# A hybrid decoder step on one core: cached keys laid out on the host, early chunk loads with filler products, and fillers in the prompt attention

## The chip, the core and the metric

The kernel runs on one core of a Trainium2 chip. The core has five engines, each with an instruction stream of its own: TensorE (PE) multiplies matrices, VectorE (DVE) and ScalarE (ACT) work on rows, GpSimd (POOL) does memsets and issues indirect transfers, SyncE (SP) issues most transfers. The streams meet only at semaphores. Transfers (DMA) bring data from the chip's memory into the on-chip memory (SBUF); PE writes into eight banks of PSUM, and DVE or ACT copy from there. The metric is the time of one execution in microseconds (us). The kernel before took 1394.13 us (median of 3 runs, 1391.05 to 1395.88).

## The reference

One layer, applied to a prompt of 512 tokens and to 8 samples of 4 tokens that each have 512 cached positions (4 pages of 128):

```
z = RMSNorm(x) @ W_in                 # 1024 -> [u 512 | q 512 | k 512 | v 512]
pool:  windowed means of u minus u, a linear per group, a scale
attn:  4 heads, each head's q and k in two halves of 64:
       (softmax(q1 k1 - slope*dist) - lambda * softmax(q2 k2 - slope*dist)) @ v, then RMSNorm
       samples attend to cache_k[page_table], cache_v[page_table] and to their new keys
h = x + [pool | attn] @ W_out
y = h + MoE(RMSNorm(h))               # 32 experts, 4 per token, clamped SwiGLU
out = RMSNorm(y); also the new pool rows, keys and values
```

cache_k has the shape (1, pages, 128 positions, 4 heads, 128 features), in float32.

## The kernel before

Everything is written by hand, engine by engine; what stands in an engine's stream is executed in that order, and nothing schedules it. The 544 tokens are five tiles (four of 128 rows, one of 32). The stages that matter here, in order of time:

**Norm and input projection.** SP loads the x tiles into two halves of `raw[:, 1]` in turn. ACT sums squares (`norm1_sums`, L740 to L745), DVE scales the rows (`norm1_rows`, L1075), PE transposes the tile (`x_transposed`, L1518), and ACT and DVE split the transposed tile into a rounded high half and a low rest (`t_hi` L758, `t_lo` L1093). The weights come in 12 chunks of 256 columns, 1024 KB each (`load_pro`, L417): 8 of W_in, 4 of W_out. A chunk is split too, by ACT (`pro_hi`, L734) into `hi` and by DVE (`pro_lo`, L1071) into `lo`, each a ring of 4 slots. A unit is one chunk by one tile: 24 products of 256 columns (`three`, L1527), high by high, high by low, low by high. PE starts unit 0 when chunk 0's low half and tile 0's low half are there. ACT copies the units' results out of PSUM, and the conversions of later chunks stand between these copies in its stream (L784). Chunks are staged in `raw[:, 0]` and `raw[:, 2]`; `raw[:, 2]` also holds xn and the gains, so chunk 2 is loaded only after all x tiles are transposed (L421).

**Prompt attention** (L1622 to L1641). 16 steps, one for each query tile and head. In step i PE makes the scores of step i + 2, waits for DVE's weights of step i (`s_a`), transposes them into PSUM bank 4 + i % 2, and multiplies the transposed weights of step i - 1 by the values. DVE adds distances, finds the maximum (L1181, L1185) and mixes the two halves (L1198); ACT takes exponentials (L883) and copies the transposed weights out (L875).

**Sample attention and output projection** (L1747 to L1777). Four sample sequences at a time: `sample_group(t)` runs over 4 heads. The cached keys come as pages with positions on partitions, so PE first transposes 16 page pieces of 128 x 128 (`page_transposes`, L1656), ACT and DVE copy two banks each into `kt_s` (L909, L1230), and `sample_scores` (L1671) multiplies. Between the two groups and after them stand pieces of the output projection (`out_product`, L1710) and the value products (`sample_values`, L1702). The pages lie in `raw`: 4 sequences at a time, 16 loads of 256 KB a set, and there are four sets: keys of sequences 0 to 3 and 4 to 7, then values of both. SP asks for the next set when the last one has been read (L469 to L472): the second keys and the first values wait for page transposes (`s_kp`), the second values for the first value products (`s_vd`).

**Router, then the experts.** The weight stream of the experts (w1 and w2, 2048 KB a load) starts when the last sample values are done (L498); up to six loads are outstanding, then each waits for PE to finish with a slot.

Of the kernel before, what the change touches and what calls it, by code (L numbers as in the profile page):

```python
# [31 lines left out]
P = 128  # L32
# [7 lines left out]
H = 4  # L40
# [122 lines left out]
def build(nc, a):  # L163
# [10 lines left out]
    with ExitStack() as ctx:  # L174
# [73 lines left out]
        kt_s = [A(A_P, 4, 512), A(A_QT, 4, 512)]  # L248
# [52 lines left out]
        s_pro = {i: sem(f"projection_weights_loaded{i}") for i in (0, 2)}  # L301
# [15 lines left out]
        s_qb, s_kp, s_sss = sem("q_blocks"), sem("page_groups_transposed"), sem("sample_score_groups")  # L317
        s_kc, s_kd, s_vd = sem("page_t_out_on_scalar"), sem("page_t_out_on_vector"), sem("sample_values_done")
# [48 lines left out]
        def pro_slot(g):  # L367
            return 2 if g >= 2 and g % 2 == 0 else 0
# [40 lines left out]
        def _(sp):  # L409
# [7 lines left out]
            def load_pro(g):  # L417
                if g == 1:
                    sp.wait_ge(s_lo, 1)
                if g == 2:  # L420
                    sp.wait_ge(s_tp, NT)  # L421
                if g >= 3:
                    sp.wait_ge(s_lo, g - 1)
                src = w_in[:, :, 256 * g:256 * g + 256] if g < 8 else w_out[:, :, 256 * (g - 8):256 * (g - 8) + 256]
                sp.dma_start(raw[:, pro_slot(g), :].rearrange("p (k n) -> p k n", k=KT), src).then_inc(s_pro[pro_slot(g)], 16)
# [23 lines left out]
            load_pro(2)  # L449
# [3 lines left out]
            for g in range(3, PRO):  # L453
                load_pro(g)
# [7 lines left out]
            def load_pages(cache, b, s):  # L462
                if s == 0:
                    sp.wait_ge(s_lo, PRO)
                if s == 1:
                    sp.wait_ge(s_po, 4)
                if s == 3:
                    sp.wait_ge(s_ust, 32)
                if s in (4, 8):  # L469
                    sp.wait_ge(s_kp, s)  # L470
                if s == 12:
                    sp.wait_ge(s_vd, 1)  # L472
                for n in range(PAGES):
                    sp.dma_start(page[:, PAGES * (s % 4) + n, :],  # L474
                                 a[cache][0][bass.ds(number[b * PAGES + n], 1)].rearrange("a t h d -> (a t) (h d)")).then_inc(s_pg[s % 4], 16)
# [79 lines left out]
        def _(pool):  # L555
            pool.memset(t_hi[:, :, NTOK:640].bitcast(F32), 0.0)
# [4 lines left out]
            pool.memset(b1_parts[:], 0.0)  # L561
# [161 lines left out]
        def _(act_e):  # L723
# [5 lines left out]
            def split_hi(slot_raw, slot, loaded):  # L729

                act_e.wait_ge(s_pro[slot_raw], loaded)
                act_e.activation(hi[:, slot, :], raw[:, slot_raw, :], ACT.Copy).then_inc(s_hi, 1)  # L732
# [168 lines left out]
            def page_t(g):  # L901

                act_e.wait_ge(s_kp, g + 1)
                if g == 1:
                    act_e.wait_ge(s_qb, 2)
                if g >= 2:
                    act_e.wait_ge(s_sss, g - 1)
                for b in range(2):
                    act_e.activation(kt_s[g % 2][:, b, :], ps[:, b, :], ACT.Copy).then_inc(s_kc, 1)  # L909

            page_t(0)
            o_square(3)
            page_t(1)
            o_root(3, P)
            page_t(2)
            o_scale(3)
            page_t(3)
            o_hi(3)
            sample_exp(0)
            for g in range(4, 8):  # L920
                page_t(g)
# [135 lines left out]
        def _(v):  # L1057
# [8 lines left out]
            def split_lo(slot_raw, slot, hi_done):  # L1066

                v.wait_ge(s_hi, hi_done)
                v.tensor_tensor(lo[:, slot, :], raw[:, slot_raw, :], hi[:, slot, :].bitcast(F32), ALU.subtract).then_inc(s_lo, 1)  # L1069

            def pro_lo(g):  # L1071
                split_lo(pro_slot(g), g % RING, g + 1)

# [150 lines left out]
            def page_t(g):  # L1224

                v.wait_ge(s_kp, g + 1)
                if g >= 2:
                    v.wait_ge(s_sss, g - 1)
                for b in range(2, 4):
                    v.tensor_copy(kt_s[g % 2][:, b, :], ps[:, b, :]).then_inc(s_kd, 1)  # L1230

            sample_queries()
            o_lo(2)
            page_t(0)
            page_t(1)
            o_recip(3)
            page_t(2)
            page_t(3)

# [73 lines left out]
            for g in range(4, 8):  # L1313
                page_t(g)
# [200 lines left out]
        def _(pe):  # L1515

            pe.wait_ge(s_g1, 32)
# [28 lines left out]
            x_transposed(1)  # L1546
            for i, (c, kind, t, part) in enumerate(UNITS):
# [95 lines left out]
            def page_transposes(g):  # L1643
# [4 lines left out]
                for b in range(4):  # L1648
                    if h == 0:
                        pe.wait_ge(s_pg[b], 64 * (t + 1))  # L1650
                    if g >= 1:
                        pe.wait_ge(s_kc if b < 2 else s_kd, 2 * g - 1 + b % 2)
                    if g == 4 and b == 2:
                        pe.wait_ge(s_he, 4)
                    for k in range(PAGES):
                        last = pe.transpose(ps[:, b, P * k:P * k + P], page[:, PAGES * b + k, P * h:P * h + P], ident)  # L1656
                last.then_inc(s_kp, 1)

            def sample_scores(g):

                t, h = g // H, g % H
                if g == 0:
                    pe.wait_ge(s_ate, 16)
                    pe.wait_ge(s_qb, 2)
# [3 lines left out]
                pe.wait_ge(s_kc, 2 * g + 2)  # L1668
                pe.wait_ge(s_kd, 2 * g + 2)
                for b in range(4):  # L1670
                    pe.matmul(ps[32 * b:32 * b + 32, B_SS + t, :], q_blk[t][:, H * b + h, :], kt_s[g % 2][:, b, :], start=h == 0, stop=h == H - 1,  # L1671
# [38 lines left out]
            def out_product(t, chunks=range(4)):  # L1710

                pe.wait_ge(s_ol, t + 1 if t < 4 else 6)
                for c in chunks:
# [3 lines left out]
                    if i < 2 or 4 <= i < 6:  # L1717
                        pe.wait_ge(s_kd, 8 + 8 * (i // 4))
# [200 lines left out]
```

## Time and profile before

| what | value |
|---|---|
| median of 3 runs | 1394.13 us |
| profiled execution, own time | 1392.96 us |
| its span, first to last instruction | 1391.2 us |
| mean granted TensorE clock | 0.972 |
| PE busy | 1306.1 us (94%) |
| DVE, ACT, POOL busy | 383.0, 269.6, 311.0 us |

The profile is of one execution. The span leaves out what lies around the first and last instruction. A timeline row gives the start, the duration, the engine, the line, the operation, the tile that is written and those read; in square brackets stands how long the engine was idle before, and what ended that. The granted clock is 1.00 at 2.4 GHz and 0.50 at 1.2 GHz; before the first change of clock that the profiler notes (22 us here), the view shows 1.00 whatever it was. PE's rows are pipelined, so the distance between starts is the price of a product, not its duration.

### The profile page before, as it was taken

Reading aid. Unit: us, or ns where it says so; the run is one execution under the profiler, and the core shown is the slowest. Engines: PE = TensorE matmul, PEld = TensorE weight load, DVE = VectorE, ACT = ScalarE, POOL = GpSimd, SP = SyncE. Lnnn points to the kernel's source line nnn. Section 1 sums busy time; section 2 is a strip of 40 time slices with the busy share of each in tenths; the row PEclk is TensorE's granted clock in tenths of the full one; section 3 lists DMA queues with packets and bytes.
Section 4 is the critical chain, followed back from the end, with each engine's and each line's share of the span. In section 5 each row is a group of like instructions: output and inputs, shape, how many; then the busy total and the mean of one; then the engine's idle time right before and its main releaser. Section 6 shows DMA issues by size and latency. Waiting matters only on the chain.

```text
span 1391.2 us, 34927 instructions
## 1 busy us (share of the span) xinstructions
PE 1306.1 (94%) x15154; PEld 702.0 (50%) x15155; DVE 383.0 (28%) x634; ACT 269.6 (19%) x586; POOL 311.0 (22%) x319
## 2 busy tenths in 40 slices
PE   5999779997998999999999999999999999999993
PEld 5999547995343333333333444555444444444442
DVE  4322584256211112222211112212111111222112
ACT  5432584132010111111111111111110100110012
POOL 1100000102613322223232222222322222222212
PEclk9999889996999999999999999999999999999997
DMA  8523404666799999999999999999999999999975
GB/s 241 149 75 124 153 1 152 242 226 278 298 412 414 388 418 417 418 415 417 416 414 412 413 416 415 416 417 415 416 412 413 414 415 415 412 415 415 409 302 163
DMA packets 76231, 472.02 MB, mean 339 GB/s; under 512 B 14638, under 2 KB 36266, under 8 KB 51505
## 3 DMA queue, kind: packets, MB, share of 16 engines
q1 hardware_dynamic: 54121, 443.38, 78.0%
q0 software_dynamic: 22064, 27.99, 7.9%
q8 instruction: 33, 0.54, 0.2%
q14 instruction: 13, 0.11, 0.0%
HBM read 457.02 MB, written 21.81 MB: 344 GB/s over the span
## 4 chain that ended last, share of the span: by engine, by line
PE 67%; DMA 22%; DVE 4%; issue 2%; ACT 2%; POOL 2%; SPq 1%; POOLq 0%; ACTq 0%; DVEq 0%
PE ps L1812 32%; PE ps L1838 18%; PE ps L1530 11%; DMA raw<-w 8%; DMA freed<-w 8%; DMA sum_rows<-arena 2%; DMA sum_rows<-arena,idx_s 1%; PE ps L1656 1%; POOL slot_table L654 1%; PE ps L1706 1%; DVE arena L1181 1%; DMA raw<-w_in 1%; DVE stats L1185 1%; SPq L474 1%; DMA raw<-cache_v 1%
## 5 line engine op out<-in xcount | busy, mean ns | idle before, releaser
L1812 PE MATMUL ps<-freed,arena 128*32 128x512 f32 x2976 | 333.2, 595 | 5.7 <-DVE arena L1370 3.2
L1812 PE MATMUL ps<-raw,arena 128*32 128x512 f32 x2976 | 333.0, 594 | 1.1 <-DMA raw<-w 1.0
L1838 PE MATMUL ps<-freed,act_t 128*32 128x256 f32 x5952 | 327.3, 379 | 2.1 <-DMA freed<-w 2.1
L1838 PEld LDWEIGHTS ps<-freed,act_t 128*32 128x32 f32 x5952 | 212.4, 110 | 126.1 <-issue 23.0
L1410 DVE TENSOR_TENSOR arena<-ps,arena 128x512 f32<-128x512 f32 x64 | 58.3, 953 | 605.6 <-PE ps L1812 605.6
L1812 PEld LDWEIGHTS ps<-freed,arena 128*32 128x32 f32 x2976 | 103.5, 110 | 212.6 <-issue 199.4
L1812 PEld LDWEIGHTS ps<-raw,arena 128*32 128x32 f32 x2976 | 100.5, 110 | 216.5 <-issue 198.3
L636 POOL DMA_INDIRECT arena<-h_rows,idx_g x87 | 91.6, 1053 | 524.7 <-issue 523.7
L646 POOL DMA_INDIRECT sum_rows<-arena,idx_s x87 | 137.3, 1578 | 100.6 <-issue 98.1
L1530 PE MATMUL ps<-hi,t_hi 128*128 128x256 f32 x400 | 116.3, 291 | 3.5 <-ACT raw L807 2.1
L1530 PE MATMUL ps<-lo,t_hi 128*128 128x256 f32 x400 | 114.5, 286 | 0.0
L1530 PE MATMUL ps<-hi,t_lo 128*128 128x256 f32 x400 | 114.5, 286 | 0.0
L988 ACT ACTIVATE arena<-arena 128x256 f32<-128x256 f32 x64 | 45.1, 704 | 275.1 <-DVE arena L1410 275.1
L1370 DVE STREAM_TRANSPOSE act_t<-arena 128x768 f32<-128x768 f32 x32 | 51.5, 1608 | 151.1 <-PE ps L1838 151.1
L978 ACT ACTIVATE arena<-ps 128x512 f32<-128x512 f32 x32 | 19.1, 597 | 378.5 <-PE ps L1820 378.5
L1530 PEld LDWEIGHTS ps<-hi,t_hi 128*128 128x128 f32 x400 | 77.9, 195 | 4.5 <-issue 4.3
L1530 PEld LDWEIGHTS ps<-lo,t_hi 128*128 128x128 f32 x400 | 78.0, 195 | 0.0
L1530 PEld LDWEIGHTS ps<-hi,t_lo 128*128 128x128 f32 x400 | 77.8, 195 | 0.0
L994 ACT ACTIVATE slot_g<-table 128x3 f32 (+1 forms) x32 | 6.6, 206 | 270.7 <-PE ps L1838 245.5
L1370 DVE STREAM_TRANSPOSE arena<-arena 128x768 f32<-128x768 f32 x32 | 51.4, 1607 | 11.7 <-DMA arena<-h_rows,idx_g 8.2
L1069 DVE TENSOR_TENSOR lo<-raw,hi 128x2048 fp32r<-128x2048 f32 x12 | 27.5, 2291 | 74.0 <-ACT hi L732 74.0
L997 ACT ACTIVATE arena<-ps,slot_g 128x256 f32<-128x256 f32 x96 | 38.6, 474 | 1.0
(259 smaller groups left out, 889.2 us busy)
## 6 DMA issues: line engine op xcount, KB each, us to landing
freed<-w SPq DMA_DIRECT2D x128, 2048.0 KB, 19.9
raw<-w SPq DMA_DIRECT2D x64, 2048.0 KB, 19.7
raw<-w_in SPq DMA_DIRECT2D x8, 1024.0 KB, 6.8
raw<-cache_k SPq DMA_DIRECT2D x32, 256.0 KB, 4.7
raw<-cache_v SPq DMA_DIRECT2D x32, 256.0 KB, 5.5
raw<-w_out SPq DMA_DIRECT2D x4, 1024.0 KB, 5.0
raw<-x_prompt SPq DMA_DIRECT2D x4, 512.0 KB, 4.0
arena<-x_prompt POOLq DMA_DIRECT2D x4, 512.0 KB, 5.8
```

Of the source, the lines that this page charges most:

```text
L474: sp.dma_start(page[:, PAGES * (s % 4) + n, :], a[cache][0][bass.ds(number[b * PAGES + n], 1)].rearrange("a t h d -> (a t) (h d)")).then_i ...
L636: pool.indirect_dma_start(out=xg[:, i, :], out_offset=None, in_=h2_quarters, in_offset=bass.IndirectOffsetOnAxis(ap=rows_of[:, i:i + 1], a ...
L646: pool.indirect_dma_start(out=y_quarters, out_offset=bass.IndirectOffsetOnAxis(ap=rows_of[:, i:i + 1], axis=0), in_=y_sb[:, i, :], in_offs ...
L978: act_e.activation(bias_t, ps[:, 7, :], ACT.Copy).then_inc(s_bt, 1)
L988: act_e.activation(dst, src[:, 0], ACT.Gelu_apprx_sigmoid).then_inc(s_s, 1)
L997: e = act_e.activation(y_sb[:, i, :], ps[:, 3 + i, 0:QD], ACT.Copy, scale=slot_g[:, i:i + 1])
L1069: v.tensor_tensor(lo[:, slot, :], raw[:, slot_raw, :], hi[:, slot, :].bitcast(F32), ALU.subtract).then_inc(s_lo, 1)
L1370: return v.transpose(dst.rearrange("p (i c t) -> p i c t", i=TT, t=TR), src.rearrange("p i (f c) -> p i c f", c=KT))
L1410: v.tensor_tensor(z1[:, lo_i:hi_i, :], ps[:, lo_i:hi_i, :], bias_t.unsqueeze(1).to_broadcast([P, hi_i - lo_i, 512]), ALU.add).then_inc(s_z ...
L1530: last = pe.matmul(out, l, r, start=start and q == 0, stop=stop and q == 2)
L1812: last = pe.matmul(ps[TR * b:TR * b + TR, i, :], x_of[:, at:at + TR], w[:, 512 * b:512 * b + 512], start=j == 0, stop=j == W1C - 1, tile_p ...
L1838: last = pe.matmul(ps[TR * b:TR * b + TR, 3 + i, 0:QD], act_of[:, at:at + TR], w[:, col:col + QD], start=g == 0 and half == 0, stop=g == W ...
```

## The change

Three things. First, the host stores each page of cache_k as features by heads by positions, (pages, 128 features, 4 heads, 128 positions), so that a loaded page has features on partitions. The page transposes, their copies and their semaphores go, and `sample_scores` reads its moving operand straight from the four pages of a sequence; the sets of loads wait for scores (`s_sss`).

Second, at the start, chunk 0 is loaded right after x tile 0; chunks 1 and 2 are loaded early into ring slots that are not yet in use (the last slot of `hi` and of `lo`, under the name `freed`), and chunk 3 follows behind the constants. ACT converts chunk 0 ahead of the second tile's sums. PE runs 34 products of a zeroed bf16 tile into bank 7 before it does anything else, and 8 after the second tile's transposes. POOL zeroes that tile first.

Third, each step of the prompt attention has 3 such products into the bank that the step's transposes write next, ahead of the wait for the weights. By then `b1_parts` holds bias parts; the fillers' results are never read.

```diff
         def pro_slot(g):
-            return 2 if g >= 2 and g % 2 == 0 else 0
+            return {0: 0, 1: 1, 2: 3}.get(g, 2 if g % 2 == 0 else 0)
+
+        def pro_raw(g):
+            return {0: raw[:, 0, :], 1: freed[:, RING - 1, :], 2: raw[:, 2, :], 3: freed[:, 2 * RING - 1, :]}[pro_slot(g)]
...
             def load_pro(g):
-                if g == 1:
+                if g == 3:
                     sp.wait_ge(s_lo, 1)
-                if g == 2:
+                if g == 4:
                     sp.wait_ge(s_tp, NT)
-                if g >= 3:
+                if g >= 5:
                     sp.wait_ge(s_lo, g - 1)
...
             load_x(0)
+            load_pro(0)
             sp.dma_start(g1, a["norm1_g"].to_broadcast([P, D])).then_inc(s_g1, 16)
+            sp.dma_start(cst[:], a["c_misc"]).then_inc(s_g1, 16)
             load_x(1)
-            sp.dma_start(cst[:], a["c_misc"]).then_inc(s_g1, 16)
-            load_pro(0)
+            load_pro(1)
+            load_pro(2)
             load_x(2)
             load_x(3)
-            load_pro(1)
             load_x(4)
...
-            load_pro(2)
+            load_pro(3)
...
                 if s in (4, 8):
-                    sp.wait_ge(s_kp, s)
+                    sp.wait_ge(s_sss, s)
...
-                                 a[cache][0][bass.ds(number[b * PAGES + n], 1)].rearrange("a t h d -> (a t) (h d)")).then_inc(s_pg[s % 4], 16)
+                                 a[cache][0][bass.ds(number[b * PAGES + n], 1)].rearrange("a p h n -> (a p) (h n)")).then_inc(s_pg[s % 4], 16)
...
+            pool.memset(b1_parts[:], 0.0).then_inc(s_warm, 1)
             pool.memset(t_hi[:, :, NTOK:640].bitcast(F32), 0.0)
...
             def pro_hi(g):
                 if g >= RING:
                     act_e.wait_ge(s_z, LAST_UNIT[g - RING])
-                split_hi(pro_slot(g), g % RING, 16 * pro_loads(g))
+                if g == RING - 1:
+                    act_e.wait_ge(s_lo, 2)
+                act_e.wait_ge(s_pro[pro_slot(g)], 16 * pro_loads(g))
+                act_e.activation(hi[:, g % RING, :], pro_raw(g), ACT.Copy).then_inc(s_hi, 1)
...
             norm1_sums(0)
+            pro_hi(0)
             for t, (_, n) in enumerate(TILES):
                 if t + 1 < NT:
                     norm1_sums(t + 1)
-                if t == 0:
-                    pro_hi(0)
...
+            def keep_warm(bank, times):
+
+                for _ in range(times):
+                    pe.matmul(ps[:, bank, :], b1_parts[:, 0:P], b1_parts[:, 0:512], start=True, stop=True)
+
+            pe.wait_ge(s_warm, 1)
+            keep_warm(7, 34)
             pe.wait_ge(s_g1, 32)
...
             x_transposed(1)
+            keep_warm(7, 8)
...
-                    pe.wait_ge(s_a, i + 1)
                     if i >= 2:
                         pe.wait_ge(s_ate, i - 1)
+                    keep_warm(4 + i % 2, 3)
+                    pe.wait_ge(s_a, i + 1)
...
-            def page_transposes(g):
...
             def sample_scores(g):
...
+                if h == 0:
+                    for b in range(4):
+                        pe.wait_ge(s_pg[b], 64 * (t + 1))
                 for b in range(4):
-                    pe.matmul(ps[32 * b:32 * b + 32, B_SS + t, :], q_blk[t][:, H * b + h, :], kt_s[g % 2][:, b, :], start=h == 0, stop=h == H - 1,
+                    pe.matmul(ps[32 * b:32 * b + 32, B_SS + t, :], q_blk[t][:, H * b + h, :], page[:, PAGES * b:PAGES * b + PAGES, P * h:P * h + P], start=h == 0, stop=h == H - 1,
                               tile_position=(0, 32 * b))
...
             def sample_group(t):
-                page_transposes(4 * t)
                 for h in range(H):
-                    if h + 1 < H:
-                        page_transposes(4 * t + h + 1)
                     sample_scores(4 * t + h)
...
+    arrays["cache_k"] = np.ascontiguousarray(arrays["cache_k"].transpose(0, 1, 4, 3, 2))
```

Line numbers in the rows below are those of each kernel's own text, so they differ between before and after for the same statement. SP's first loads, before (x_prompt: x tiles, norm_g: gains, c_misc: constants, w_in: a chunk):

```order
2 L415 DMA raw<-x_prompt 128x1024
3 L428 DMA raw<-norm_g 128x1024
4 L415 DMA raw<-x_prompt 128x1024
5 L430 DMA cst<-c_misc 128x822
6 L425 DMA raw<-w_in 128x8x256
7 L415 DMA raw<-x_prompt 128x1024 [waits xn_done] x2
8 L425 DMA raw<-w_in 128x8x256 [waits lo_done]
```

The same place on SP in the changed kernel:

```order
2 L417 DMA raw<-x_prompt 128x1024
3 L427 DMA raw<-w_in 128x8x256
4 L431 DMA raw<-norm_g 128x1024
5 L432 DMA cst<-c_misc 128x822
6 L417 DMA raw<-x_prompt 128x1024
7 L427 DMA freed<-w_in 128x8x256 x2
8 L417 DMA raw<-x_prompt 128x1024 [waits xn_done] x2
```

A chunk now stands ahead of gains and constants, and two more ahead of x tile 2.

ACT's first instructions, before (the first operation of each pair sums squares, the second takes the root; `hi` is a chunk's high half):

```order
3 L743 ACTIVATE arena,stats<-raw 128x1024
4 L745 ACT_TABLE_LOAD
5 L745 ACTIVATE stats<-stats,cst 128x1
6 L743 ACTIVATE arena,stats<-raw 128x1024
7 L745 ACTIVATE stats<-stats,cst 128x1
8 L732 ACTIVATE hi<-raw 128x2048
9 L758 ACTIVATE t_hi<-ps 128x8x128
```

The same place on ACT in the changed kernel:

```order
3 L744 ACTIVATE arena,stats<-raw 128x1024
4 L746 ACT_TABLE_LOAD
5 L746 ACTIVATE stats<-stats,cst 128x1
6 L738 ACTIVATE hi<-raw 128x2048
7 L744 ACTIVATE arena,stats<-raw 128x1024
8 L746 ACTIVATE stats<-stats,cst 128x1
9 L758 ACTIVATE t_hi<-ps 128x8x128
```

The conversion of chunk 0 has moved ahead of the second tile's sums. DVE's order there is the same in both: rows of tile 0, rows of tile 1, chunk 0's low half, tile 0's low half.

PE from the last steps of the prompt attention to the output projection, before (the 128x128 products from `raw` are page transposes, the 32x512 ones the scores):

```order
1017 L1640 MATMUL ps<-arena 128x128 x4
1018 L1616 MATMUL ps<-cst,arena 128x128 x4
1019 L1640 MATMUL ps<-arena 128x128 x4
1020 L1656 MATMUL ps<-cst,raw 128x128 x32
1021 L1671 MATMUL ps<-arena 32x512 x4
1022 L1674 MATMUL ps<-arena 32x32 x4
1023 L1656 MATMUL ps<-cst,raw 128x128 x16
1024 L1671 MATMUL ps<-arena 32x512 x4
1025 L1674 MATMUL ps<-arena 32x32 x4
1026 L1656 MATMUL ps<-cst,raw 128x128 x16
```

The same place on PE in the changed kernel, with the last filler triple:

```order
1033 L1486 MATMUL ps<-b_parts 128x512 x3
1034 L1605 MATMUL ps<-cst,arena 128x128 x4
1035 L1615 MATMUL ps<-arena 128x128 x4
1036 L1590 MATMUL ps<-cst,arena 128x128 x4
1037 L1615 MATMUL ps<-arena 128x128 x4
1038 L1632 MATMUL ps<-raw,arena 32x512 x4
1039 L1635 MATMUL ps<-arena 32x32 x4
1040 L1632 MATMUL ps<-raw,arena 32x512 x4
1041 L1635 MATMUL ps<-arena 32x32 x4
1042 L1632 MATMUL ps<-raw,arena 32x512 x4
```

The scores of a group now stand back to back; 128 transposes have gone in the two groups together.

## Rows read from the trace of the kernel before

**Rows 1.** The page's chain that ended last, share of the span by engine.

```profile
PE 67%; DMA 22%; DVE 4%; issue 2%; ACT 2%; POOL 2%; SPq 1%; POOLq 0%; ACTq 0%; DVEq 0%
```

**Rows 2.** Stretches: start:end, length, then busy us by engine, clock, DMA, GB/s.

```profile
42.30:145.00 102.70, 102.11 (x822) 101.05 (x822) 32.17 (x27) 37.63 (x52) 5.16 (x8) 0.98 0.33 107
158.80:209.50 50.70, 36.68 (x185) 24.09 (x186) 43.58 (x116) 42.28 (x126) 0.98 (x2) 0.80 0.13 47
...
330.00:340.00 10.00, 8.45 (x134) 6.18 (x135) 3.07 (x8) 0.06 (x1) 3.31 (x3) 0.50 0.52 213
340.00:350.00 10.00, 7.70 (x51) 2.33 (x53) 8.56 (x19) 0.00 (x0) 3.90 (x4) 0.67 0.11 31
...
410.00:420.00 10.00, 10.00 (x100) 3.77 (x96) 0.00 (x0) 0.60 (x1) 0.00 (x0) 1.00 1.03 440
```

**Rows 3.** The start: timeline, DMA rate in 40 slices of 0 to 16 us, chain.

```profile
3.11 1.81 POOL L561 MEMSET b_parts<- 128x2048 bf16 x1
...
9.01 1.06 ACT L743 ACTIVATE arena<-raw 128x1024 f32<-128x1024 f32 x1 [3.01 <-DMA cst<-c_misc]
...
13.04 1.90 ACT L732 ACTIVATE hi<-raw 128x2048 fp32r<-128x2048 f32 x1
...
13.46 1.28 DVE L1081 SCALAR_TENSOR_TENSOR arena<-raw,stats 128x1024 f32<-128x1024 f32 x1
...
14.96 2.29 DVE L1069 TENSOR_TENSOR lo<-raw,hi 128x2048 fp32r<-128x2048 f32 x1 [0.22 <-ACT hi L732]
...
GB/s 0 0 0 0 41 164 348 276 338 328 338 287 225 225 277 420 420 406 407 392 369 390 384 381 348 353 323 156 10 0 0 0 0 0 0 61 113 297 317 471
...
18.54 4.75 PE ps L1530 x24
24.16 2.88 PE ps L1530 x24
```

**Rows 4.** Chunk 2's conversion on ACT's timeline; PE's wait behind it.

```profile
40.01 1.91 ACT L732 ACTIVATE hi<-raw 128x2048 fp32r<-128x2048 f32 x1 [7.66 <-DMA raw<-w_in]
...
PE ps L1530 <- ACT raw L807: 2.1, 1, 2.1
```

**Rows 5.** Prompt attention: waits (us, times, longest), a DVE row; a slow product.

```profile
PE ps L1630 <- DVE arena L1198: 13.2, 14, 2.4
...
DVE arena L1181 <- PE ps L1610: 2.2, 3, 0.9
...
174.08 1.02 DVE L1181 SCALAR_TENSOR_TENSOR arena<-arena,ps 128x384 f32<-128x384 f32 x2 [0.95 <-PE ps L1610]
...
332.17 0.43 PE ps L1846
```

**Rows 6.** The chain through the sample attention: start, us, what.

```profile
209.56 1.76 PE ps L1656 x16
...
214.01 0.99 PE ps L1671 x8
...
223.10 11.51 PE ps L1530 x96
234.61 1.76 PE ps L1656 x16
...
247.56 14.59 PE ps L1530 x120
...
265.56 4.55 PE ps L1706 x160
...
270.13 0.33 SPq L474
...
285.76 4.58 PE ps L1706 x160
```

**Rows 7.** SP's first value loads; DMA rate, 40 slices of 244 to 266 us.

```profile
245.00 8.34 SPq L474 DMA_DIRECT2D raw<-cache_v  x16
...
GB/s 30 0 0 108 331 205 399 372 354 298 272 324 413 380 365 350 387 391 406 428 398 421 413 421 400 397 332 283 339 372 406 369 376 231 41 26 15 0 0 0
```

More of the change, by code:

```diff
@@ L300, in build @@
         s_late = sem("pool_inputs_loaded")
-        s_pro = {i: sem(f"projection_weights_loaded{i}") for i in (0, 2)}
+        s_pro = [sem(f"projection_weights_loaded{i}") for i in range(4)]
+        s_warm = sem("filler_zeroed")
         s_raw = [sem(f"raw_pair_loaded{i}") for i in range(RAW // 2)]
@@ L316, in build @@
         s_pg = [sem(f"pages_loaded{i}") for i in range(4)]
-        s_qb, s_kp, s_sss = sem("q_blocks"), sem("page_groups_transposed"), sem("sample_score_groups")
-        s_kc, s_kd, s_vd = sem("page_t_out_on_scalar"), sem("page_t_out_on_vector"), sem("sample_values_done")
+        s_qb, s_sss, s_vd = sem("q_blocks"), sem("sample_score_groups"), sem("sample_values_done")
         s_smx, s_se, s_sa, s_ptr, s_pe = (sem(n) for n in ("sample_max", "sample_exp", "sample_weights", "sample_wt", "sample_wt_out"))
@@ L417, in load_pro @@
             def load_pro(g):
[L418 removed]
+                if g == 3:
                     sp.wait_ge(s_lo, 1)
[L420 removed]
+                if g == 4:
                     sp.wait_ge(s_tp, NT)
[L422 removed]
+                if g >= 5:
                     sp.wait_ge(s_lo, g - 1)
                 src = w_in[:, :, 256 * g:256 * g + 256] if g < 8 else w_out[:, :, 256 * (g - 8):256 * (g - 8) + 256]
[L425 removed]
+                sp.dma_start(pro_raw(g).rearrange("p (k n) -> p k n", k=KT), src).then_inc(s_pro[pro_slot(g)], 16)
             load_x(0)
+            load_pro(0)
             sp.dma_start(g1, a["norm1_g"].to_broadcast([P, D])).then_inc(s_g1, 16)
+            sp.dma_start(cst[:], a["c_misc"]).then_inc(s_g1, 16)
             load_x(1)
[L430 to L431 removed]
+            load_pro(1)
+            load_pro(2)
             load_x(2)
             load_x(3)
[L434 removed]
             load_x(4)
@@ L452, in _ @@
             sp.dma_start(pw, a["pool_w"][0].rearrange("g c e -> c g e")).then_inc(s_late, 16)
-            for g in range(3, PRO):
+            for g in range(4, PRO):
                 load_pro(g)
@@ L560, in _ @@
             pool.memset(bias_r[:].bitcast(F32), 0.0)
-            pool.memset(b1_parts[:], 0.0)
             pool.memset(rank[:], -1.0)
@@ L727, in gate_exp @@
                 act_e.activation(gate[0:n, t, :], top[0:n, 0:4], ACT.Exp, bias=st[0:n, 44:45], accum_out=st[0:n, 45:46]).then_inc(s_ge, 1)
-            def split_hi(slot_raw, slot, loaded):
-                act_e.wait_ge(s_pro[slot_raw], loaded)
-                act_e.activation(hi[:, slot, :], raw[:, slot_raw, :], ACT.Copy).then_inc(s_hi, 1)
             def pro_hi(g):
@@ L899, in sample_exp @@
                 act_e.activation(s_smp[:, t, :], s_smp[:, t, :], ACT.Exp, bias=st[:, 32 + t:33 + t], accum_out=st[:, 34 + t:35 + t]).then_inc(s_se, 1)
[L901 to L911, printed above, removed]
             o_square(3)
-            page_t(1)
             o_root(3, P)
-            page_t(2)
             o_scale(3)
-            page_t(3)
             o_hi(3)
             sample_exp(0)
-            for g in range(4, 8):
-                page_t(g)
             sample_exp(1)
@@ L1064, in link @@
                 v.wait_ge(s_dve, chain[0])
-            def split_lo(slot_raw, slot, hi_done):
-                v.wait_ge(s_hi, hi_done)
-                v.tensor_tensor(lo[:, slot, :], raw[:, slot_raw, :], hi[:, slot, :].bitcast(F32), ALU.subtract).then_inc(s_lo, 1)
             def pro_lo(g):
-                split_lo(pro_slot(g), g % RING, g + 1)
+                v.wait_ge(s_hi, g + 1)
+                if g == RING - 1:
+                    v.wait_ge(s_lo, RING - 1)
+                v.tensor_tensor(lo[:, g % RING, :], pro_raw(g), hi[:, g % RING, :].bitcast(F32), ALU.subtract).then_inc(s_lo, 1)
             def norm1_rows(t):
@@ L1223, in _ @@
                     o_lo(i // 4 - 2)
[L1224 to L1230, printed above, removed]
             sample_queries()
             o_lo(2)
-            page_t(0)
-            page_t(1)
             o_recip(3)
-            page_t(2)
-            page_t(3)
             def sample_softmax(t):
@@ L1312, in _ @@
             residual(0)
-            for g in range(4, 8):
-                page_t(g)
             sample_softmax(1)
@@ L1641, in _, with sample_scores @@
                     last.then_inc(s_pv, 1)
-            def page_transposes(g):
+            def sample_scores(g):
                 t, h = g // H, g % H
@@ L1647, in page_transposes @@
                     pe.wait_ge(s_sb, 16)
[L1648 to L1662, printed above, removed]
                     pe.wait_ge(s_ate, 16)
```

5 lines of the change are left out of this document (removed).

## The prediction

> **What bounds the kernel now.** I read the page's chain of waits first, then a table of busy times by stage, then the timelines and the waits of the stages that the change touches. The chain is PE for 67% of the span and DMA for 22% [rows 1]. The reader is to see two regimes in it. From about 380 us on, the experts run with PE and the DMA rings both full (in 410 to 420 us PE is busy 10.00 of 10 and the DMA share is 1.03), while just ahead of that, at 340 to 350 us, the DMA share is 0.11: the weight stream there waits for the routing that follows from all that lies before [rows 2]. The stream's first load waits for the last sample values, so a microsecond taken out of the first 290 us moves both the stream and PE's first expert, and should come off the end one for one. The change lies wholly in these 290 us, in three places.
>
> **Start: chunk loads and the first fillers.** Before, ACT starts when the constants land, at 9.01 us [rows 3]. Ahead of them in SP's queue stood 512 KB three times (two of x, one of gains); now it is one x tile, chunk 0 (1024 KB) and the gains, so 512 KB more. At the 369 to 390 GB/s that the DMA row shows at 8 to 9 us [rows 3] that is 1.4 us later; if chunk 0 delayed them by its whole length it would be 2.8. The Trainium skill (DMA: Bandwidth & Descriptors, Bandwidth) times a lone 1 MB load at 6.15 us; by that the constants would be 6.15 us late in place of 1.4, and the total 4.7 us higher. The trace moves the same chunk behind other loads at nearly full rate, so I stay with the row.
>
> ACT now converts chunk 0 to its high half (1.90 us) ahead of the second tile's sums. That tile's norm on DVE ended at 13.46 + 1.28 = 14.74 us and now ends 1.90 later, at 16.64; DVE's low half of chunk 0 stands behind it and began at 14.96, so it moves by 1.7 [rows 3]. PE's first projection unit then starts at 18.54 + 1.4 + 1.7 = 21.6 us. In exchange it should find the clock up: the first 24 products took 4.75 us, the next 24 took 2.88 [rows 3]. So the first unit ends at 24.5 in place of 23.3: 1.2 us lost. The 34 fillers begin after POOL's memset of their operand (1.81 us [rows 3], and now POOL's first), which I put near 2.6 us. The trace has no 128-row product of 512 bf16 columns; from 0.12 us for 256 columns at the upper level (2.88/24) I take 0.24 each there, and 0.43 at the lower (a 512-column product at 332 us, granted clock 0.50 in that stretch [rows 5]). They end between 10.8 and 17.2 us, the transposes of tile 0 become ready at 13.5 + 1.4 = 14.9, so there may be gaps of some 3 us and the clock may have fallen again by the time of the 8 later fillers. These cost nothing at 0.24, since PE waits for DVE's low half anyway; at 0.43, with slow transposes ahead, they end about 23.4 and the first unit at 28.2: 4.9 us lost.
>
> The early loads give something back. ACT waited 7.66 us for chunk 2 before converting it at 40.01, but PE lost only 2.1 us by it, because the evacuations queued behind that conversion became late only then [rows 4]. The stall goes: chunk 2 is now staged in a ring slot and lands some 15 us before it is read. What was late next, chunk 3, is asked for at about 30 us and read after 45. The clock fell after that stall: a mean of 0.98 over 102.7 us [rows 2] is 3 to 5 us at half speed, of which I take 3.4, worth 1.7. Together 3.8 us back. The start is therefore worth between 3.8 - 1.2 = 2.6 and 3.8 - 4.9 = -1.1; since a gap of 2.1 us was already followed by a fall, I do not take the upper end but +1.
>
> **Prompt attention: 48 fillers.** PE stood idle 13.2 us in front of the 14 weight transposes that waited for DVE [rows 5]. 48 fillers take 11.5 us at 0.24 and 20.6 at 0.43. At the upper level they fit in idle time; what is queued behind them (transposes, value products, the scores two heads ahead) has a whole step of slack, since DVE works on the next head meanwhile. At the lower they put 20.6 - 13.2 = 7.4 us on the chain. The gain is what DVE lost to slow scores: 2.2 us in 3 waits, the longest 0.95 at 174.08 [rows 5], in a stage whose mean granted clock was 0.80 [rows 2]. But the first scores wait for DVE, as before, so the clock may fall before the first filler stands, and the first steps then carry fillers at 0.43: about 1.3 us each against 0.9 of idle time a step, for some steps. I set this against the gain and take 0, with -7.4 and +2.2 as ends. DVE and ACT keep their own work (DVE 43.58 of 50.7 us busy [rows 2]), so there is no more to win.
>
> **Sample attention: no page transposes.** This is the large term. Each of 8 head groups loses 16 page transposes (1.76 us for the first) and two copies each on ACT and DVE; what remains is the scores, 0.99 us a group [rows 6]. PE work falls from 223.10 - 209.56 = 13.5 us to about 5 in the first half (four groups, 4.0, and about 1 for the output transposes that wait for ACT), and from 247.56 - 234.61 = 12.95 to 4.0 in the second. If nothing else bound, that is 8.5 + 9 = 17 us.
>
> But the pages are loaded into four slots in turn, and a load is now released by the last scores of the group before, not by its transposes. So the freed time turns into waits. A set of 16 page loads (4.2 MB) takes from 270.13 to 285.76 us when it is alone: 15.6 us, at the end of which the last value products start at once [rows 6]. The first value set, beside POOL's loads of x, takes from 245.00 to 264.4 (the last slice with bytes in it): 19.4 [rows 7]. Step by step on the old time axis:
> - scores of the first half end at 209.56 + 4.0 = 213.6;
> - the second key set lands at 213.6 + 15.6 = 229.2, while PE has finished the first output product (11.51) at about 226: a new wait of 3 us;
> - scores of the second half end at 233.2;
> - the first value set lands at 233.2 + 19.4 = 252.6; PE's work up to there (265.56 - 247.56 = 18.0) ends at 251.2: a wait of 1.4;
> - values take 4.55, to 257.2, and release the last set, which lands at 257.2 + 15.6 = 272.8.
> The second values start at 272.8 in place of 285.76: 13.0 us gained. Ends: 17 if no load is late, 10 if the clock falls after the 3 us wait (1.7 us, as after the stall above) and the value set takes a microsecond longer. The moving operand of the scores now lies in four pieces of 128 columns; no row has that form, the nearest is the same product from one piece, and I take its time.
>
> **Sum.** 1 + 0 + 13.0 = 14.0 us. The profiled execution took 1392.96 us, so 1379.0; the median of the runs shown is 1.2 us above it, and I state 1380.
>
> **Rivals.**
> - Forecast, 1380 us, chance 0.62, its own range 1374 to 1385: the page loads bind the sample stage.
> - No late pages and a clock that stays up, about 1371 us (17 + 2.6 + 2.2 = 21.8 off), 0.15. For it: POOL's x loads now come earlier against the value set, and the same bytes may overlap better. Against it: the last set alone already ends the chain at 285.76 in the trace.
> - Fillers at the lower level, about 1388.5 us (13.0 - 1.1 - 7.4 = 4.5 off), 0.15. For it: the granted clock was 0.80 in this stage, and at 330 to 340 us a PE that was busy 8.45 of 10 us stayed at 0.50 [rows 2]. Against it: fillers at the lower level leave PE no idle time, and in 410 to 420, never idle, it had 1.00 [rows 2].
> - Slower: the fillers make PE the bound of the whole prompt attention at 1.2 GHz. PE was busy 36.68 us at mean 0.80 [rows 2], which is 58.7 at 0.50, and with 20.6 us of fillers 79.3 in a stage of 50.7: 28.6 added, 14 saved elsewhere, so about 1407 us, 0.04. It decides once PE's work there exceeds the stage by 14 us; against it stands the same row of 410 to 420 us.
> - The change does not reach the end: the prelude shortens, but the weight stream and not the routing sets the first expert, about 1393 us, 0.04. Against it is the DMA share of 0.11 ahead of the experts.
>
> **How the numbers follow.** 1371 to 1388 leaves out a part of the cold-filler case, the last two, and the far end of the best one, under 2 in 10. A measurement of this kernel can tell 0.3%, 4.2 us, from no change: faster means below 1390. The first two cases and most of the third lie there: 0.90. Within 0.3%: 0.06; slower 0.04.
>
> **What would show it.** Right: PE's first unit near 21.6 us, no wait for chunk 2, the first sample scores back to back, then PE waiting for cache_k pages for some 3 us and for both cache_v sets, and the second values starting some 14 us earlier. Wrong: a first unit past 24 us; DVE waiting for scores behind fillers in a stage longer than 50.7 us; no DMA wait ahead of the second scores (then the gain is nearer 20); or score groups well over 1 us, which would mean that the operand in pieces is slow.

## The result

The changed kernel took 1376.41 us (median of 4 runs, 1374.96 to 1379.19), the kernel before 1393.06 in the same job (4 runs, 1391.05 to 1395.88). The ratio is 0.9894, its 95% interval 0.9866 to 0.9923: faster, by 14.8 us if the ratio is put on 1393.06 (10.7 to 18.7 by its interval; the two medians are 16.7 apart). A second job gave 0.9883 (0.9867 to 0.9899). The forecast was 1380.

The two profiled executions took 1392.96 and 1379.19 us, 13.8 apart, beside 14.0 in the sum; that of the changed kernel was the slowest of its four. The table has the stages of both, each from the start of PE's first product in it.

| stage | before, us | after, us | difference | in the sum |
|---|---|---|---|---|
| up to the first attention product | 156.38 | 155.64 | -0.74 | -1 |
| prompt attention | 53.19 | 53.76 | +0.57 | 0 |
| end of attention to second sample values | 76.20 | 64.63 | -11.57 | -13.0 |
| second values to the first expert product | 57.66 | 55.59 | -2.07 | 0 |
| experts and end | 1047.8 | 1047.8 | 0.0 | 0 |

The last row answers the question of the stream: what was saved ahead of the experts came off the end whole. That the difference is 0.0 to the tenth is chance, since over all the runs below this stage took between 1044.5 and 1049.4 us. The page's chain after (shares of the span by engine) stands against [rows 1]:

```profile
PE 66%; DMA 22%; DVE 3%; issue 2%; ACT 2%; SPq 2%; POOL 2%; POOLq 0%; DVEq 0%; ACTq 0%
```

The start after, against [rows 3]: ACT and DVE on the timeline, then PE, whose last two rows are from the chain:

```profile
10.27 1.06 ACT L744 ACTIVATE arena<-raw 128x1024 f32<-128x1024 f32 x1 [4.18 <-DMA cst<-c_misc]
...
12.93 1.89 ACT L738 ACTIVATE hi<-raw 128x2048 fp32r<-128x2048 f32 x1
...
19.82 1.22 DVE L1074 TENSOR_TENSOR t_lo<-ps,t_hi 128x1024 fp32r<-128x1024 f32 x1
...
2.64 9.53 PE L1486 MATMUL ps<-b_parts 128*128 128x512 bf16 x34 [2.64 <-POOL b_parts L559]
14.76 1.06 PE L1497 MATMUL ps<-cst,raw 128*128 128x128 f32 x8 [2.59 <-DVE raw L1062]
...
19.95 3.19 PE L1486 MATMUL ps<-b_parts 128*128 128x512 bf16 x7 [0.22 <-issue]
...
23.14 3.23 PE ps L1503 x24
27.25 2.88 PE ps L1503 x24
```

ACT starts 1.26 us later than before. The 34 fillers end at 12.17; PE then waits 2.59 us for the first transposes. The low half of tile 0 is ready at 21.04 us, but 8 fillers (7 of them have records here), 0.43 us apart, stand ahead of the unit until 23.14: the granted clock was 0.50 from 17.00 to 23.83 us.

The busy time by stretch after, columns as in [rows 2]: the start, two parts of the projection, the prompt attention, the sample attention up to and behind the second key set, and the stage ahead of the experts:

```profile
13.40:22.60 9.20, 5.68 (x24) 3.71 (x25) 7.52 (x8) 7.34 (x12) 0.00 (x0) 0.70 0.70 234
...
42.30:145.00 102.70, 102.15 (x834) 100.97 (x833) 30.36 (x26) 37.22 (x51) 5.27 (x9) 1.00 0.30 99
...
155.60:209.40 53.80, 43.65 (x243) 24.63 (x252) 45.23 (x121) 42.57 (x128) 0.98 (x2) 0.94 0.16 56
...
213.40:229.40 16.00, 12.17 (x100) 11.97 (x101) 4.62 (x11) 3.55 (x7) 0.00 (x0) 0.98 0.83 293
229.40:234.60 5.20, 5.17 (x65) 1.80 (x65) 0.00 (x0) 0.00 (x0) 0.00 (x0) 0.75 0.00 0
...
274.04:329.63 55.59, 45.00 (x688) 41.68 (x689) 33.07 (x109) 17.83 (x39) 7.27 (x10) 0.86 0.70 276
```

The clock before the first unit is 0.70, that of the projection 1.00 in place of 0.98, that of the attention 0.94 in place of 0.80 with DVE still busy 45 of 54 us. Behind the wait for keys it is 0.75 for the 5.2 us of the second scores.

The waits of PE up to 340 us (us, times, longest), against [rows 4, 5], and the chain through the sample attention, against [rows 6]:

```profile
PE ps L1605 <- DVE arena L1179: 7.0, 8, 1.8
...
PE ps L1632 <- DMA raw<-cache_k: 3.1, 1, 3.1
...
PE ps L1664 <- DMA raw<-cache_v: 1.8, 2, 1.2
```

```profile
209.41 1.00 PE ps L1632 x8
210.47 0.86 PE ps L1632 x8
...
222.34 6.95 DMA raw<-cache_k
229.43 1.94 PE ps L1632 x8
231.47 1.21 PE ps L1632 x8
...
243.88 9.78 DMA raw<-cache_v
253.80 4.61 PE ps L1664 x160
...
266.75 7.16 DMA raw<-cache_v
274.04 4.57 PE ps L1664 x160
```

No wait for chunk 2 is left. A score group on its four pieces takes 0.86 to 1.00 us at the upper level, as before, so the form costs nothing that shows. At each set the chain passes through a load of pages, as forecast.

### The profile page after: what moved, and what is told of

It reads as the page before. It is cut to its first block, busy times and chain, and to the rows that moved or that the text cites. A ratio compares the mean times of both kernels' runs of the same rounds, so it can differ in the third digit from the quotient of the medians.

```text
span 1377.4 us, 34777 instructions
## 1 busy us (share of the span) xinstructions
PE 1303.8 (95%) x15110; PEld 666.7 (48%) x15117; DVE 368.1 (27%) x618; ACT 252.4 (18%) x570; POOL 312.9 (23%) x319
## 4 chain that ended last, share of the span: by engine, by line
PE 66%; DMA 22%; DVE 3%; issue 2%; ACT 2%; SPq 2%; POOL 2%; POOLq 0%; DVEq 0%; ACTq 0%
PE ps L1768 33%; PE ps L1794 18%; PE ps L1503 9%; DMA raw<-w 8%; DMA freed<-w 8%; DMA sum_rows<-arena 2%; SPq L477 2%; DMA raw<-cache_v 1%; POOL slot_table L657 1%; PE ps L1664 1%; PE ps L1632 1%; DMA arena<-h_rows,idx_g 1%; DMA cst<-c_misc 1%; DMA raw<-cache_k 1%; DVE arena L1162 0%
## 5 line engine op out<-in xcount | busy, mean ns | idle before, releaser
L1794 PEld LDWEIGHTS ps<-freed,act_t 128*32 128x32 f32 x5952 | 202.7, 110 | 136.6 <-issue 24.4
L1376 DVE TENSOR_TENSOR arena<-ps,arena 128x512 f32<-128x512 f32 x64 | 58.3, 953 | 602.4 <-PE ps L1768 602.4
L1768 PEld LDWEIGHTS ps<-freed,arena 128*32 128x32 f32 x2976 | 97.9, 110 | 221.8 <-issue 206.9
L1768 PEld LDWEIGHTS ps<-raw,arena 128*32 128x32 f32 x2976 | 94.6, 110 | 221.4 <-issue 201.0
L972 ACT ACTIVATE arena<-arena 128x256 f32<-128x256 f32 x64 | 37.2, 581 | 276.3 <-DVE arena L1376 276.3
L1054 DVE TENSOR_TENSOR lo<-raw,hi 128x2048 fp32r<-128x2048 f32 x10 | 22.9, 2291 | 68.7 <-ACT hi L738 68.7
```

The source lines that it names most:

```text
L972: act_e.activation(dst, src[:, 0], ACT.Gelu_apprx_sigmoid).then_inc(s_s, 1)
L1054: v.tensor_tensor(lo[:, g % RING, :], pro_raw(g), hi[:, g % RING, :].bitcast(F32), ALU.subtract).then_inc(s_lo, 1)
L1376: v.tensor_tensor(z1[:, lo_i:hi_i, :], ps[:, lo_i:hi_i, :], bias_t.unsqueeze(1).to_broadcast([P, hi_i - lo_i, 512]), ALU.add).then_inc(s_z ...
L1768: last = pe.matmul(ps[TR * b:TR * b + TR, i, :], x_of[:, at:at + TR], w[:, 512 * b:512 * b + 512], start=j == 0, stop=j == W1C - 1, tile_p ...
L1794: last = pe.matmul(ps[TR * b:TR * b + TR, 3 + i, 0:QD], act_of[:, at:at + TR], w[:, col:col + QD], start=g == 0 and half == 0, stop=g == W ...
```

## The experiments

Theory A was that of the prediction: the page loads bind the sample stage, and the rest of the change is worth little. The rivals say that the gain comes from fillers and clock, or that PE's work is what is left. Ratios are to the kernel before on the same chip, each with its 95% interval; stage times are those of the profiled execution.

**The layout alone.** Loads, ring and ACT's order as before, no fillers:

```diff
-            load_pro(0)
             sp.dma_start(g1, a["norm1_g"].to_broadcast([P, D])).then_inc(s_g1, 16)
+            load_x(1)
             sp.dma_start(cst[:], a["c_misc"]).then_inc(s_g1, 16)
-            load_x(1)
-            load_pro(1)
-            load_pro(2)
+            load_pro(0)
...
-            keep_warm(7, 34)
...
-            keep_warm(7, 8)
...
-                    keep_warm(4 + i % 2, 3)
```

> Only the host layout and the scores read from it; start order, chunk loads and fillers are as in the kernel before. Theory A (the layout carries nearly all of the gain): the time from the last product of the prompt attention to the second value products is 64 to 66 us, as in the changed kernel (64.6) and not as before (76.2); the first unit starts at 18.5 us; total 1377 to 1382 us. Rival B (the early loads and the fillers carry a real part, 4 us or more): total 1384 us or more.

Measured: 1378.59 us, ratio 0.9906 (0.9889 to 0.9923), 2.2 us above the changed kernel's median, which the two intervals do not tell apart. Attention at 154.75 us and 54.83 long, sample stage 63.44, a little under the 64 to 66 expected. So the layout carries nearly all of the gain. The first unit on PE's chain:

```profile
18.50 3.11 PE ps L1497 x24
```

From its end to the attention this kernel needs 133.14 us, the kernel before 133.09 and the changed kernel 129.27: the early loads and the warmer clock do give 3.9 us. But the first unit ended 4.8 us before the changed kernel's (21.61 against 26.37), so the new start as a whole loses 0.9 us against this kernel. Up to that unit PE does the same as in the kernel before, where the unit took 4.75 us from 18.54 on [rows 3]; here it took 3.11, with no filler ahead of it. The first rise of the clock in the trace comes at 17.1 us here and at 22.2 there, so these two executions differ in how slow the first unit is, though no filler tells them apart.

**No fillers in the attention.**

```diff
-                    keep_warm(4 + i % 2, 3)
```

> The changed kernel without the 48 fillers of the prompt attention. Theory A (they are worth nothing): the attention stage, 53.8 us with them, is 52.5 to 54.5 us, its mean granted clock falls back from 0.94 to about 0.8, and the total stays within 2 us of 1376.4. Rival B (the higher clock is worth something): stage over 55 us, total 1378.5 or more. Rival C (the fillers stand in the way): stage under 52.5 us, total under 1374.5.

Measured: 1374.94 us, ratio 0.9887 (0.9867 to 0.9907). The attention took 53.80 us, with fillers 53.76. The stretch of the attention:

```profile
154.09:207.90 53.81, 36.30 (x200) 24.07 (x204) 45.22 (x121) 42.83 (x128) 0.98 (x2) 0.84 0.17 57
```

The clock is 0.84 in place of 0.94, PE 7.35 us less busy, and DVE's 45.22 and ACT's 42.83 us are nearly the same, as theory A has it. The fillers raise the clock where the clock does not set the end.

**No fillers at the start.**

```diff
-            pe.wait_ge(s_warm, 1)
-            keep_warm(7, 34)
...
-            keep_warm(7, 8)
```

> The changed kernel without the 34 + 8 fillers at the start, the early chunk loads kept. Theory A (the 8 fillers hold up the first unit as much as the clock gives back): the first unit starts at about 21.1 us in place of 23.1, takes up to 4.8 us in place of 3.2 and ends within 0.8 us of 26.4; the attention starts within 1.5 us of 155.6; total within 2 us of 1376.4. Rival B (without them PE stays at the lower level through several units): attention starts 2 us or more later. Rival C (they only hold it up): attention starts 1.5 us or more earlier.

Measured: 1375.51 us, ratio 0.9891 (0.9872 to 0.9910). The first two steps of PE's chain, and the attention:

```profile
21.28 5.05 PE ps L1501 x24
26.34 0.87 PE ps L1495 x8
```

```profile
155.60:208.19 52.59, 41.28 (x243) 23.37 (x252) 45.20 (x121) 42.71 (x128) 0.99 (x2) 1.00 0.17 58
```

Without fillers the first unit starts 1.86 us earlier, at the moment that its operand is ready, runs cold, and ends at 26.33; with them it ends at 26.37. What they give to the unit they took ahead of it (theory A). In this execution the attention had a clock of 1.00 and 52.59 us, the shortest seen: 1.2 us below that at 0.94. Its 48 fillers are those of the changed kernel, and why its clock did not fall is not shown.

**A quarter of each page.** The output leaves the other three quarters of the cached keys and values out:

```diff
-    sp.dma_start(page[:, PAGES * (s % 4) + n, :],
+    sp.dma_start(page[:, PAGES * (s % 4) + n, 0:128],
...
```

> The changed kernel with a quarter of each page loaded (128 of 512 columns); three quarters of the cached keys and values are left out, so the sample outputs are not the reference's. Theory A (the page loads bind the sample stage after the change): PE's waits for cache_k (3.1 us) and cache_v (1.8 us) and the clock's fall behind the first go, and the second values start 59 to 61 us after the attention's end in place of 64.6; total lower by 4 to 6 us. Rival B (other engines' work, ACT's and DVE's softmax chain, is as late as the pages): the waits change their name, and the stage stays over 63 us.

Measured: 1369.82 us in one run, sample stage 58.34, a little past the 59 to 61 expected. PE waits for no load in it; rows of its chain:

```profile
214.77 11.52 PE ps L1503 x96
226.28 0.99 PE ps L1632 x8
...
248.10 4.50 PE ps L1664 x160
...
267.73 4.50 PE ps L1664 x160
```

The second scores begin as the output product ends, 3.1 us earlier than in the changed kernel. With the loads out of the way PE is the bound, 6.3 us below. So the loads do bind the stage of the changed kernel, and 6.3 us is what they cost beyond PE's work.

**Constants first.** ACT's conversion of chunk 0 goes back behind the second tile's sums, 14 fillers stand in place of 8, and SP's order is

```diff
             load_x(0)
+            sp.dma_start(cst[:], a["c_misc"]).then_inc(s_g1, 16)
+            sp.dma_start(g1, a["norm1_g"].to_broadcast([P, D])).then_inc(s_g1, 16)
+            load_x(1)
             load_pro(0)
-            sp.dma_start(g1, a["norm1_g"].to_broadcast([P, D])).then_inc(s_g1, 16)
-            sp.dma_start(cst[:], a["c_misc"]).then_inc(s_g1, 16)
-            load_x(1)
             load_pro(1)
-            load_pro(2)
             load_x(2)
             load_x(3)
+            load_pro(2)
             load_x(4)
```

> The changed kernel with another start: constants and gains are loaded ahead of chunk 0, chunk 2 behind x tile 3, ACT converts chunk 0 after the second tile's sums as in the kernel before, and 14 fillers in place of 8 stand behind the second transposes. Theory A (the first unit is late because the constants stand behind chunk 0 and ACT's conversion ahead of the second tile's sums): ACT starts at 7.3 to 8 us in place of 10.3, the first unit starts at 17 to 18 us in place of 22.6, the attention starts at 150 to 152 us in place of 155.6, and the total falls by 3 to 5 us. Rival B (the x tiles behind the chunks set the pace of the first five units, so a unit that starts earlier waits longer): attention not before 154.5 us, total within 2 us of 1376.4.

Measured: 1373.09 us, ratio 0.9865 (0.9834 to 0.9897). PE's and ACT's timelines at the start:

```profile
13.28 1.06 PE L1498 MATMUL ps<-cst,raw 128*128 128x128 f32 x8 [1.78 <-DVE raw L1063]
14.58 1.09 PE L1498 MATMUL ps<-cst,arena 128*128 128x128 f32 x8 [0.24 <-DVE arena L1063]
15.73 2.97 PE L1487 MATMUL ps<-b_parts 128*128 128x512 bf16 x13
18.66 0.36 PE L1504 MATMUL ps<-hi,t_hi 128*128 128x256 f32 x1
...
8.78 1.06 ACT L744 ACTIVATE arena<-raw 128x1024 f32<-128x1024 f32 x1 [2.83 <-DMA raw<-norm_g]
...
13.14 1.92 ACT L738 ACTIVATE hi<-raw 128x2048 fp32r<-128x2048 f32 x1 [0.23 <-DMA raw<-w_in]
```

ACT starts 1.5 us earlier than in the changed kernel, the conversion no longer stands ahead of the second sums, the transposes come soon after the fillers, and the first unit starts at 18.66 at the upper clock: it ends at 21.77. ACT and the unit are both later than expected (7.3 to 8 and 17 to 18 us). The attention starts at 151.02, as expected, 4.6 us earlier than in the changed kernel; the median is 3.3 us lower. The first unit ends where it does with the layout alone (21.61), and the early loads' 3.9 us behind it are kept. Several things were changed together here (constants, chunk 2, ACT's order, the number of fillers), and no run separates them; by the traces ACT's earlier start makes up 1.5 of the 4.6 us.

**The wait for keys filled.** 13 more fillers between the output product and the second scores, in the changed kernel and in the one with the constants first.

```diff
             out_product(0)
+            keep_warm(0, 13)
             sample_group(1)
```

> The changed kernel with 13 more fillers between the first output product and the second score group, where PE waits 3.1 us for cache_k pages. Theory A (the wait is for loads alone and costs a fall of the clock besides): no low clock at 228 us, the four score groups take 3.6 us in place of 4.9, the time from the first second-group score to the first values is the same (23.5 to 24.4 us). Rival B: the fillers run past the landing of the pages and delay the second scores by over 0.5 us.

> The start of the kernel with constants first and the 13 fillers ahead of the second scores together. Theory A: the gains add, total 1371 to 1373 us, below both kernels. Rival B (the start's gain is eaten by x tiles, the clock's by the load chain): 1375 us or more.

Measured: 1378.70 us in one run, and 1373.11, ratio 0.9867 (0.9839 to 0.9895). The chain of the first:

```profile
226.46 2.75 PE ps L1486 x12
229.22 0.99 PE ps L1632 x8
230.27 0.86 PE ps L1632 x8
...
253.30 4.57 PE ps L1664 x160
...
272.99 4.50 PE ps L1664 x160
```

The clock does not fall, the score groups take 0.99 and 0.86 us in place of 1.94 and 1.21, as theory A has it, and the second scores end 1.6 us earlier. The first values start only 0.5 us earlier and the second 1.1, and no total is lower: the gains did not add in the second kernel. There the clock fell at the first values instead (6.24 us in place of 4.6), and the stage was 65.03 us long against 64.17.

**No fillers at all**, the omissions of the second and third experiment together.

> The changed kernel without any filler: layout and early chunk loads alone. Theory A (fillers are worth nothing in sum): attention starts within 1.5 us of 155.6, the attention stage is 52.5 to 55 us, total within 3 us of 1376.4. Rival B (they hold the clock up where it counts): total 1380 or more.

Measured: 1375.26 us in one run; first unit at 21.29 us, 5.31 long, attention 54.07 at a clock of 0.81, sample stage 61.91. In this run nothing is lost without the 90 products (theory A).

**The decision between the versions.** The changed kernel once more, the constants first once more, and the latter without its three kinds of fillers, in one job:

```diff
-            keep_warm(7, 34)
...
-            keep_warm(7, 14)
...
-                    keep_warm(4 + i % 2, 3)
```

> The changed kernel itself, once more, so that the next two can be set against it on the same chip. Expected by every theory: 1375 to 1379 us; attention starts at 155.6 us, the second sample values 64 to 65 us after its end.

> The order of loads with the constants first, as in e5, beside the changed kernel in the same job. Theory A (what comes earlier in the first 290 us comes off the end one for one): attention starts 4.6 us earlier (151.0), and the total is 3.5 to 5 us below the changed kernel's. Theory B (the expert stage gives part of it back, the totals differ by run to run changes of the clock): less than 2 us below.

> e10 without any filler product. Theory A (fillers are paid where they stand in front of the first unit, and bring something where that unit would begin cold with nothing held up): the first unit starts at 18.5 us but takes 4.8 to 5.3 us instead of 2.9, so the attention starts 2 us later than in e10 and the total is 2 us higher. Theory B (fillers are worth nothing here either): attention starts within 0.7 us of e10's, total within 1 us. The attention itself 53.5 to 54.5 us long by both.

| kernel | median, us | lowest to highest | ratio to before, interval |
|---|---|---|---|
| the changed kernel | 1376.22 | 1375.44 to 1377.44 | 0.9883, 0.9867 to 0.9899 |
| constants first | 1372.74 | 1372.40 to 1373.84 | 0.9858, 0.9841 to 0.9874 |
| the same, no fillers | 1373.29 | 1370.77 to 1378.06 | 0.9853, 0.9835 to 0.9871 |

The kernel with the constants first is 3.5 us better: all four runs lie below the lowest of the changed kernel. Its attention began at 151.29 us against 155.36; of these 4.1 us, 3.5 reach the end by the medians, at the lower edge of theory A. It is faster than both the kernel before and the changed kernel.

Without fillers the first unit, at 18.97 us in PE's chain, took 4.34 us against 3.06, less than the 4.8 to 5.3 expected:

```profile
18.97 4.34 PE ps L1502 x24
23.32 1.16 PE ps L1496 x8
24.48 2.87 PE ps L1502 x24
```

The attention began 1.6 us later, nearer to theory A, and was 55.83 us long at a clock of 0.80, past the 54.5 expected and the longest of all; but the medians differ by 0.55 us, as theory B has it, and the profiled execution was the slowest of its four. With the layout alone the first unit took 3.11 us without any filler. Whether fillers are worth anything in this order stays open: the four totals without them lie 7.3 us apart.

## Why the prediction was right, step by step

- **Sample stage, 13.0 in the sum, 11.6 measured.** Counted from the end of the attention, the second keys landed after 20.0 us (forecast 19.6), PE waited 3.1 us (3), the first values started after 44.4 (43.0), the second after 64.6 (63.2). The last set took 15.6 us from the end of the first values (253.80 + 4.61 to 274.04), as before. In this trace the term was over-sized mainly by one thing, which stood only as the lower end: the clock fell behind the wait, and the second scores took 5.2 us in place of 4.0. With the wait filled they took 3.8, and the second values started 1.1 us earlier. The rest is within what executions differ by: the same stage took 63.4 to 65.8 us in the six in which the clock fell at that wait, the changed kernel's two among them, and 61.8 to 61.9 in three in which it did not (no fillers in the attention, none at the start, none at all). In those three the second keys also landed earlier, 18.6 to 18.7 us after the attention against 18.9 to 20.0; why is not shown. The mechanism itself was shown by the short pages: the waits went and the stage fell to 58.3.
- **Start, 1 in the sum, 0.74 in this pair of traces; the sign is not shown.** ACT began at 10.27 us (10.4 forecast). The data of the first unit were ready at 21.04, half a microsecond ahead of the 21.6, but the unit began at 23.14: the fillers were neither at the upper level nor hidden. It ended at 26.37, inside the 24.5 to 28.2 and 3.1 later than before. In the kernel without the attention's fillers, which has the same start, the clock was back at 20.78 us and the unit ended at 24.82. With 0.74 gained in all, the projection gave back 3.8, as forecast, and 3.9 against the kernel with the layout alone. But the sum took the slow first unit of the one trace before (4.75 us) as the rule for the old start. With the layout alone the old start had it in 3.11 us, and against that kernel the new start loses 0.9. That +1 and +0.74 agree is thus luck. The constants came 1.26 us later with 512 KB more ahead of them (a chunk in, an x tile out), near the 1.4 of the row's rate. The 6.15 us of the Trainium skill (DMA: Bandwidth & Descriptors, Bandwidth), weighed there, is for a whole 1 MB transfer issued from GpSimd. As a delay in SP's queue it does not show here.
- **Attention, 0 in the sum, +0.57 in this trace.** The fillers cost no time and give none that can be told: with them the stage took 52.59 to 53.79 us over eight profiled executions, without them 53.19 to 55.83 over five. PE's wait for DVE fell from 13.2 to 7.0 us [rows 5], so it was filled and not moved. The rival of cold fillers (1388.5) is out: in the changed kernel the first steps alone were cold.
- **Not in the sum: 2.1 us from the second values to the first expert.** The clock there was 0.86 in place of the 0.79 of the kernel before:

```profile
285.76:343.42 57.66, 47.63 (x688) 43.12 (x689) 32.93 (x109) 17.96 (x39) 7.25 (x10) 0.79 0.68 266
...
319.20:346.50 27.30, 19.91 (x320) 13.76 (x324) 17.18 (x55) 3.44 (x10) 6.59 (x7) 0.50 0.61 255
```

  The same 688 products were busy 47.63 us then and 45.00 now; before, the last 24 us of the stage ran at 1.2 GHz without a break. In the other kernels the stage took 53.2 to 55.9 us, those without fillers among them, and their clock there was 0.83 to 0.90. Why is not shown: there is one trace of the kernel before, and no run changed this stage alone.

So the mechanism of the large term was right, and the total missed by 3.6 us of 1380. In the traces the terms missed by 0.3, 0.6 and 1.4, all on the side of less gain, and the 2.1 us that nothing forecast made up for them. The closeness of 13.8 to 14.0 is therefore luck, the more so as the trace after is of the slowest run. The totals of the rivals (1371, 1388.5 and 1407) were counted from the profiled 1392.96 without the 1.2 us that 1380 includes; no choice between them turns on it. The rival without late pages (1371) is answered by PE's waits for pages and not by the total, which lies between it and the forecast.

## What to carry to other kernels

Work that leaves an engine is worth the time until the next transfer becomes late, so follow the buffers' releases step by step on the old time axis, and count from the end of the last reader; here that gave the landing of the second keys to within half a microsecond, and what followed the first cold products to within 1.4. The rearrangement of the cached keys is done on the host, outside the time measured. None of the fillers here was shown to pay: in the attention another engine set the end, and at the start they held up what stood behind them. So look at which engine ends a stage, and at what is queued behind, before adding any. And of several first loads, put first the small one that everything waits for, and let a large one that only a later step reads follow it; the faster order here did so, though other things were changed with it.

## What was not expected of the hardware

- At the wait for keys the clock fell in the changed kernel (3.1 us idle) and with the layout alone (1.9 us idle), and stayed in the one without the start's fillers (1.7 us idle). With that wait filled it stayed at 1.00 there, and also behind the 2.3 us that PE then waited for values. The idle time alone thus does not tell in these runs when it falls. Filling the wait moved the first values by only 0.5 us, since the transfer behind them sets their start.
- The first unit of the same old start took 4.75 us in one execution and 3.11 in another, with no filler ahead of it in either.
- 48 fillers in the attention left the first steps cold all the same: in the changed kernel the clock was at 0.50 for 6.8 us from 156.9 on, and at 1.00 for the rest of the stage; the execution without the start's fillers had 1.00 throughout.
